# Two stacked transformer blocks on one core: grouped output products in a delta rule, first triangular blocks turned by TensorE, and waits placed elsewhere

## The reference, cut to what matters

```python
m = jnp.where(strict, jnp.einsum('bnhid,bnhjd->bnhij', kb, kc) * decay, 0.0)
...
sol = lax.linalg.triangular_solve(m, rhs, left_side=True, lower=True, unit_diagonal=True)
...
def step(state, xs):
    qd, kd, a, uu, ww, cd = xs
    v_new = uu - jnp.einsum('bhck,bhkv->bhcv', ww, state)
    o = jnp.einsum('bhck,bhkv->bhcv', qd, state) + jnp.einsum('bhij,bhjv->bhiv', a, v_new)
    state = state * cd[..., None, None] + jnp.einsum('bhck,bhcv->bhkv', kd, v_new)
    return state, o
```

## Time and profile before

| what | value |
|---|---|
| median of 3 runs | 2355.02 us (2354.6 to 2356.83) |
| profiled execution, its own time | 2357.62 us |
| its span, first to last instruction | 2355.8 us |
| TensorE busy | 2193.8 us (93%) |
| GpSimd busy | 1499.3 us (64%) |
| ScalarE busy | 1070.5 us (45%) |
| VectorE busy | 949.8 us (40%) |
| mean granted TensorE clock | 0.962 |

### The profile page before, as it was taken

One profiled execution on the slowest core, in us unless ns is written; L12 is line 12 of the kernel. 1 busy time (PEld: TensorE's weight loads), 2 busy tenths in 40 slices (PEclk: granted clock), 3 DMA queues, 4 the chain that ended last, 5 costly groups with the idle time before them and its releaser, 6 DMA issues.

```text
span 2355.8 us, 36004 instructions
## 1 busy us (share of the span) xinstructions
PE 2193.8 (93%) x15336; PEld 2010.8 (85%) x15336; DVE 949.8 (40%) x1528; ACT 1070.5 (45%) x1505; POOL 1499.3 (64%) x632
## 2 busy tenths in 40 slices
PE   7989989899878989989999899898999989998997
PEld 6779977799778879879899899888788789998997
DVE  4352356422375546375112211456374661123113
ACT  4555555455545252245444444462532444544443
POOL 6588876698844233356778688663243556686885
PEclk9999999999988989999999999999999999999999
DMA  8345534355522222243445455432122344454553
GB/s 326 126 161 183 193 116 161 108 197 181 185 92 102 68 70 77 72 143 129 149 164 186 143 186 190 143 126 83 61 90 72 116 139 158 144 179 147 193 179 117
DMA packets 47184, 333.06 MB, mean 141 GB/s; under 512 B 5168, under 2 KB 5552, under 8 KB 7856
## 3 DMA queue, kind: packets, MB, share of 16 engines
q1 hardware_dynamic: 47024, 330.76, 40.6%
HBM read 329.69 MB, written 1.05 MB: 140 GB/s over the span
## 4 chain that ended last, share of the span: by engine, by line
PE 61%; DVE 7%; ACT 3%; issue 1%; POOL 0%; ACTq 0%; DVEq 0%
PE bank L146 14%; PE bank L147 13%; PE bank L148 13%; PE y L146 2%; PE y L148 2%; PE y L147 2%; PE bank L1675 2%; PE bank L1611 1%; PE bank L1685 1%; PE bank L1729 1%; PE bank L1728 1%; DVE conv L1325 1%; PE bank L1684 1%; DVE sc L2285 1%; PE bank L1506 1%
## 5 line engine op out<-in xcount | busy, mean ns | idle before, releaser
L336 POOL TENSOR_TENSOR w_lo<-w_raw,w_hi 128x1024 fp32r<-128x1024 f32 x602 | 1465.7, 2440 | 831.7 <-ACT w_hi L327 831.7
L327 ACT ACTIVATE w_hi<-w_raw 128x1024 fp32r<-128x1024 f32 x602 | 636.4, 1059 | 1066.9 <-PE bank L148 896.3
L146 PE MATMUL bank<-x_hi,w_hi 128*128 128x256 f32 x2960 | 881.4, 298 | 34.0 <-POOL w_lo L336 19.3
L147 PE MATMUL bank<-x_lo,w_hi 128*128 128x256 f32 x2960 | 852.5, 288 | 0.0
L148 PE MATMUL bank<-x_hi,w_lo 128*128 128x256 f32 x2960 | 851.8, 288 | 0.0
L146 PEld LDWEIGHTS bank<-x_hi,w_hi 128*128 128x128 f32 x2960 | 583.3, 197 | 58.6 <-issue 24.3
L147 PEld LDWEIGHTS bank<-x_lo,w_hi 128*128 128x128 f32 x2960 | 583.4, 197 | 10.5 <-issue 8.6
L148 PEld LDWEIGHTS bank<-x_hi,w_lo 128*128 128x128 f32 x2960 | 582.7, 197 | 0.0
L862 DVE SCALAR_TENSOR_TENSOR conv<-bank,par_sb,conv 128x254 f32<-128x254 f32 (+1 forms) x176 | 76.8, 477 | 251.8 <-ACT conv L850 250.2
L1188 DVE TENSOR_TENSOR hid_lo<-hid,hid_hi 128x512 fp32r<-128x512 f32 x22 | 45.1, 2048 | 247.0 <-ACT hid_hi L1183 247.0
L146 PE MATMUL y<-w_hi,hid_hi 128*128 128x512 f32 x352 | 139.4, 396 | 1.2 <-DVE hid_lo L884 1.2
(11 more groups left out here) (393 smaller groups left out, 3279.8 us busy)
## 6 DMA issues: line engine op xcount, KB each, us to landing
w_raw<-w SPq DMA_DIRECT2D x300, 1024.0 KB, 4.8
ln_rows<-ln_rows SPq DMA_DIRECT2D x4, 1024.0 KB, 5.7
mem_tok<-mem SPq DMA_DIRECT2D x2, 1024.0 KB, 7.0
const_sb<-const SPq DMA_DIRECT2D x1, 1536.0 KB, 9.4
par_sb<-par SPq DMA_DIRECT2D x2, 553.5 KB, 10.7
xn<-xT SPq DMA_DIRECT2D x1, 1024.0 KB, 5.0
w_raw<-w SPq DMA_DIRECT2D x2, 512.0 KB, 5.3
x_tok<-x SPq DMA_DIRECT2D x1, 1024.0 KB, 8.5
```

Source lines behind the costliest of these rows:

```text
L146: pe.matmul(out, lhs[0], rhs[0], start=start, stop=False, skip_group_check=skip)
L147: pe.matmul(out, lhs[0], rhs[1], start=False, stop=False, skip_group_check=skip)
L327: act.activation(self.hi[:, h % HALVES, :], self.raw[:, n % RAWS, i * HW:(i + 1) * HW], ACT.Copy).then_inc(*sig.up("high", h))
L336: pool.tensor_tensor(self.lo[:, h % HALVES, :], self.raw[:, n % RAWS, i * HW:(i + 1) * HW], self.hi[:, h % HALVES, :].bitcast(F32), ALU.su ...
```

## The change

- In each output block of the scan the four heads' products with the state come first, then the four products with `vn`; only the first is marked as the start of an accumulation.
- The spread is two steps, `spread` (waits for the second key logarithm) and `spread_e` (waits for the fourth), with stream between them. Half 1's steps start one position later.
- `ti` (identity minus the first level of the triangle) is finished on DVE in the steps g0 and g1. TensorE turns `ti` instead of `mt`, and ScalarE copies the turned block to `t`, in place of three operations on DVE per group (one of them on `ti`, now made earlier).
- The gap before `tail0` is 4 instead of 2. ScalarE's table load and logarithms of the tail stand one position before `tail0`, instead of directly behind the last chunk.
- In the second mixer DVE's `normalise` of groups 0 and 1 stands ahead of `index_sum(1)`. The memory values' units and the gates and branches behind them use the banks in another order.
- In the first mixer the spread stands one half later, `scores(0)` and `turn(0)` one position later.

```diff
@@ -523,7 +523,7 @@
 
-        main.pe(pe, self.at(5))
+        main.pe(pe, self.at(6))
         if l == 0:
@@ -569,7 +569,7 @@
 
-        main.pe(pe, self.at(13))
+        main.pe(pe, self.at(13) + 1)
         pe.wait_ge(*sig.at("roped", l, 1))
@@ -582,7 +582,7 @@
         scores(3)
-        main.pe(pe, self.at(17))
+        main.pe(pe, self.at(17) + 1)
         turn(0)
@@ -1447,10 +1447,11 @@
         for c in range(2):
-            token_unit(f"mv{c}", m["mv"][:, :, c * HALF:(c + 1) * HALF], [4 + 2 * c, 5 + 2 * c], m["mn"])
+            token_unit(f"mv{c}", m["mv"][:, :, c * HALF:(c + 1) * HALF], [6 - 2 * c, 7 - 2 * c], m["mn"])
+        u["mv0"].need = u["mv0"].need + [("o_low", l, 1, 3)]
         for n in range(4):
-            gate_unit(1, n, 4)
-            branch_unit(1, n, 5)
+            gate_unit(1, n, 6)
+            branch_unit(1, n, 7)
         u["wb10"].need = u["wb10"].need + [("o_low", l, 1, 3)]
@@ -1465,7 +1466,7 @@
         self.units = [u[n] for n in self.order]
-        self.steps = [self.places(0, 30), self.places(1, 72)]
+        self.steps = [self.places(0, 30), self.places(1, 73)]
 
@@ -1479,10 +1480,10 @@
 
-        gaps = ([("spread", 0), ("k0", 4 if hf == 0 else 2), ("k1", 1), ("v0", 1), ("v1", 1), ("q0", 1), ("q1", 1), ("beta", 1),
+        gaps = ([("spread", 0), ("spread_e", 2 if hf == 0 else 1), ("k0", 2 if hf == 0 else 1), ("k1", 1), ("v0", 1), ("v1", 1), ("q0", 1), ("q1", 1), ("beta", 1),
                  ("g0", 1), ("g1", 1), ("lower", 2)] + [(f"{n}{lv}", 1) for lv in range(1, 6) for n in ("y", "c")]
                 + [("solved", 1)] + [(f"{n}{c}", g) for c in range(NCH) for n, g in (("w", 2), ("o", 1))]
-                + [("tail0", 2), ("tail1", 1)])
+                + [("tail0", 4), ("tail1", 1)])
         at, out = start, {}
@@ -1625,12 +1626,15 @@
         if hf == 0:
-            pe.wait_ge(*sig.at("key_logged", l, 0, 3))
+            pe.wait_ge(*sig.at("key_logged", l, 0, 1))
             pe.wait_ge(*sig.at("decays", l))
         else:
-            pe.wait_ge(*sig.at("key_logged", l, 1, 3))
+            pe.wait_ge(*sig.at("o_dn", l, 0, 0))
+        spread(m["rowq"][:, 1, :], 0).then_inc(*sig.up("spread_g", l, hf))
+        main.pe(pe, self.step_at(hf, "spread_e"))
+        pe.wait_ge(*sig.at("key_logged", l, hf, 3))
+        if hf:
             pe.wait_ge(*sig.at("o_dn", l, 0, 1))
-        spread(m["rowq"][:, 1, :], 0).then_inc(*sig.up("spread_g", l, hf))
         spread(m["ge_row"][:, :], 2).then_inc(*sig.up("spread_e", l, hf))
@@ -1663,14 +1667,14 @@
         for g in range(2):
-            pe.wait_ge(*sig.at("mt_made", l, hf, g))
+            pe.wait_ge(*sig.at("begun", l, hf, g))
             for n in range(4 * g, 4 * g + 4):
-                mm = pe.transpose(yd[g][:, (n % 4) * P:(n % 4 + 1) * P], h["mt"][:, n, :], K("ident"))
-            mm.then_inc(*sig.up("lower", l, hf, g, 0))
+                mm = pe.transpose(yd[g][:, (n % 4) * P:(n % 4 + 1) * P], h["ti"][:, n, :], K("ident"))
+            mm.then_inc(*sig.up("begun_turned", l, hf, g))
         for lv in range(1, 6):
             for g in range(2):
-                pe.wait_ge(*sig.at("kept", l, hf, g, lv - 1))
+                pe.wait_ge(*(sig.at("kept", l, hf, g, lv - 1) if lv > 1 else sig.at("t_begun", l, hf, g)))
                 for n in range(4 * g, 4 * g + 4):
@@ -1724,9 +1728,11 @@
             for hh in range(4):
-                cols = slice(hh * P, (hh + 1) * P)
-                pe.matmul(op[r, cols], h["qd"][:, hh, c * CH:(c + 1) * CH], h["st"][:, c % 2, hh, :], start=True, stop=False)
-                mm = pe.matmul(op[r, cols], h["at"][r, tt * 4 + hh, r], h["vn"][r, hh, :], start=False, stop=True)
+                pe.matmul(op[r, hh * P:(hh + 1) * P], h["qd"][:, hh, c * CH:(c + 1) * CH], h["st"][:, c % 2, hh, :],
+                          start=hh == 0, stop=False, skip_group_check=True)
+            for hh in range(4):
+                mm = pe.matmul(op[r, hh * P:(hh + 1) * P], h["at"][r, tt * 4 + hh, r], h["vn"][r, hh, :],
+                               start=False, stop=True, skip_group_check=True)
             mm.then_inc(*sig.up("o_done", l, hf, c))
@@ -1908,6 +1914,11 @@
         act.activation(h["e"][:, :, :], h["e"][:, :, :], ACT.Exp).then_inc(*sig.up("decay_made", l, hf))
+        main.act(act, self.step_at(hf, "lower"))
+        for g in range(2):
+            act.wait_ge(*sig.at("begun_turned", l, hf, g))
+            act.activation(h["t"][:, 4 * g:4 * g + 4, :], bank[g][:, :].rearrange("p (n i) -> p n i", n=4), ACT.Copy
+                           ).then_inc(*sig.up("t_begun", l, hf, g))
         main.act(act, self.step_at(hf, "solved"))
@@ -1927,6 +1938,7 @@
                                ).then_inc(*sig.up("o_squared", l, hf, tt))
+        main.act(act, self.step_at(hf, "tail0") - 1)
         act.preload_act_table_set("natural_log_exp_and_others")
@@ -2050,9 +2062,9 @@
         main.dve(dve, self.at(64))
-        self.index_sum(dve, 1)
         self.normalise(dve, 0)
         self.normalise(dve, 1)
+        self.index_sum(dve, 1)
         self.index_mask(dve, 1, {1: 66, 4: 69, 6: 70})
@@ -2179,6 +2191,11 @@
             dve.tensor_tensor(h["mt"][:, pr, :], heads(tt), h["es"][:, pr, :], ALU.mult).then_inc(*sig.up("mt_made", l, hf, tt))
+            dve.wait_ge(*sig.at("mt_made", l, hf, tt))
+            step(dve.tensor_tensor(h["ti"][:, pr, :], h["mt"][:, pr, :], K("level0T").unsqueeze(1).to_broadcast([P, 4, P]),
+                                   ALU.mult))
+            dve.tensor_tensor(h["ti"][:, pr, :], K("ident").unsqueeze(1).to_broadcast([P, 4, P]), h["ti"][:, pr, :],
+                              ALU.subtract).then_inc(*sig.up("begun", l, hf, tt))
 
@@ -2190,21 +2207,7 @@
 
-        for g in range(2):
-            pr = slice(4 * g, 4 * g + 4)
-            dve.wait_ge(*sig.at("mt_made", l, hf, g))
-            dve.tensor_tensor(h["ti"][:, pr, :], h["mt"][:, pr, :], K("level0T").unsqueeze(1).to_broadcast([P, 4, P]), ALU.mult
-                              ).then_inc(*sig.up("begun", l, hf, g))
         main.dve(dve, self.step_at(hf, "lower"))
-        for g in range(2):
-            pr = slice(4 * g, 4 * g + 4)
-            dve.wait_ge(*sig.at("begun", l, hf, g))
-            dve.tensor_tensor(h["ti"][:, pr, :], ident, h["ti"][:, pr, :], ALU.subtract)
-            dve.wait_ge(*sig.at("lower", l, hf, g, 0))
-            dve.tensor_tensor(h["t"][:, pr, :], four(g), lev[:, 0:1, :].to_broadcast([P, 4, P]), ALU.mult
-                              ).then_inc(*sig.up("masked2", l, hf, g, 0))
-            dve.wait_ge(*sig.at("masked2", l, hf, g, 0))
-            dve.tensor_tensor(h["t"][:, pr, :], ident, h["t"][:, pr, :], ALU.subtract).then_inc(*sig.up("kept", l, hf, g, 0))
         for lv in range(1, 6):
@@ -2216,7 +2219,7 @@
                 dve.wait_ge(*sig.at("cross", l, hf, g, lv))
-                dve.wait_ge(*sig.at("kept", l, hf, g, lv - 1))
+                dve.wait_ge(*(sig.at("kept", l, hf, g, lv - 1) if lv > 1 else sig.at("t_begun", l, hf, g)))
                 ins = dve.tensor_tensor(h["ti"][:, pr, :], h["ti"][:, pr, :], four(2 + g), ALU.subtract)
```

## The result

The changed kernel takes 2334.78 us (median of 4 runs, 2333.98 to 2336.76), the kernel before beside it on the same chip 2355.93 us: ratio 0.99, 95% interval 0.9884 to 0.9917. It is faster by about 21 us by the medians and by 23.6 us by the ratio (interval 19.6 to 27.3) where 56 were forecast, and 2334.8 lies outside the range of 2280 to 2326. The profiled execution of after took 2335.5 us (span 2333.4), 22.1 less than that of before.

The account below looks back on a forecast made before the run. TensorE, busy 93% of the span, bounds it by matmuls, waits and lower clock. Terms 13.5 + 11 + 14.1 + 2.9 - 4 - 1 + 10.1 + 3.5 + 6.0 = 56.1 us give 2299; range 2280 to 2326.

Parts of the forecast that it names:

- the first triangular blocks: Start of the triangular solve: turning a finished `ti` cuts waits from 13.0 to 2.9, plus 4 of clock: 14.1 us gained.
- the tail: Chain's end, `tail0` four positions behind: +2.9 us, less 4 at the index scores and 1 at half 1's rotations.
- the prediction's own signs of being wrong: Blocks keeping 0.36 us a product, 1.2 GHz behind shortened waits, or DVE waits beyond 3 us inside y and c steps.
- Grouping: Scan's 16 output blocks: one change of shape instead of seven, 2.88 to 2.04 us each, 13.5 us gained.
- Index order: Normalise ahead of the second index sum: 10.5 of wait and 4.8 of clock gone, new waits at `merged`; 10.1 us gained.
- First model: Spread a half later, scores and turn one position later: 6.0 us gained, with 3.0 lost at L512.
- Memory banks: Memory values in banks 6 and 7: the wait for mk3's copy goes, 3.5 us gained.
- Spread: Split spread, first group needing only the second key logarithm: wait 8.9 to 3.9, plus 6 of clock, 11 us gained.
- Clock: Time regained from TensorE's 1.2 GHz stretches behind waits that shrink or vanish, 19.8 us over all terms.
- waits move more than they vanish: Rival, chance 0.22: DVE is slow beside GpSimd at every named place, costing 17 us more, 2316 us.

Follow-up runs that it names:

- 8: The changed kernel with both the old tail (gap 2, logarithms straight behind the last chunk) and the old solve start (`mt` turned): 2313.65 us.
- 1: The kernel before with only the output products of the scan grouped: 2351.82 us.
- 9: The changed kernel with the new `ti` operations reading the Gram block in PSUM instead of SBUF, first triangular level left out: 2315.57 us.
- 10: The changed kernel with the old tail and three GpSimd weight subtractions a layer held back until DVE's steps are done: 2300.07 us.
- 11: As 10, but the second half's chain starts at position 72 as before, not 73: 2313.72 us.
- 6: The changed kernel with the old tail: gap 2 before `tail0`, table load and logarithms directly behind the last chunk: 2319.60 us.
- 3: The kernel before with only the spread split over two steps, the first waiting for the second key logarithm: 2349.25 us.
- 2: The kernel before with only both normalise steps moved ahead of the second index sum: 2347.83 us.
- 7: The changed kernel with the old solve start (`mt` turned, three DVE operations behind it, no ScalarE copy): 2325.17 us.
- 5: The kernel before with only the later tail: `tail0` four positions behind the last block, table load and logarithm one position ahead: 2386.93 us.

## Why the prediction was wrong

In the terms of the table the forecast had 13.5 for the work, 22.8 for waits and 19.8 for the clock. Measured, before against after: 2114.8 - 2103.6 = 11.2, 149.6 - 138.6 = 11.0, and half of 0.3 for the clock. Two steps make nearly all of the miss, the first triangular blocks and the tail: the forecast had 14.1 - 2.1 = 12 us gained for both, and undoing both (8) shows that they cost 18.8, 31 of the 32.5 us between forecast and measured gain. How the 31 divide depends on the order of undoing. Of the prediction's own signs of being wrong none came as written: the blocks take 2.04 us, the clock came back behind the shortened spread, and the wait beyond 3 us stands one step ahead of the y steps.

- **Grouping, 13.5: right.** 11.1 alone, 10.7 by the bookkeeping of single executions, 14.0 with the clock taken out of all of them. That the change of shape was the cost is argued, as said under 1. The Trainium skill, "TensorEngine Tiling (Array Packing)", "Key Properties", says that changing the tiling mode drains TensorE and gives no price; the blocks here agree with it, at 0.84 us for seven changes that became one.
- **Index order, 10.1: right** (8.7), with the new wait of 2.35 a layer where 2.1 stood. **First model, 6.0: right in sum** (6.8), wrong at L512, where DVE's shorter operation gave back what the forecast took, and wrong in the clock's 5.1, which did not come. **Memory banks:** the wait behind `mk` is gone as said; not run alone.
- **Spread, 11: measured 7.5.** The wait fell by 5.0 as forecast, and the clock gave about the 6 forecast (14 us less at 1.2 GHz between the medians); some 3 us came back, which no run explains.
- **First triangular blocks, 14.1: the step with the largest error in the changed kernel.** Undoing it gains 11.3, so it is off by 25; with the old tail it costs 0.5. The text priced the new operations as hidden, with "uncovered it costs up to 1 us a half, 4 in all". It had the right row, a pair of 3.26 us beside GpSimd, and placed it wrongly: it timed the last group's pair and its turn, and took the first group's to be clear. In the trace both groups meet a subtraction (2.78 and 2.72), the first one also delays the second group's `mt`, and TensorE waits 0.55 + 3.4 us in half 0 and 2.2 in half 1: 12.3 in all, 9.4 more than forecast. Runs 9 and 10 remove the wait in two different ways, by the operand's place and by GpSimd's timing, with DVE's list unchanged in number and order.
- **Tail, +2.9 - 4 - 1 = -2: the other step that failed.** Alone it costs 26.6 us, in the changed kernel 18.3, with the old solve start 7.5. Its own waits were sized right (z 6.2 as forecast, turns 8.1 against 7.0). Three things are off. The 5.5 us behind iq go by the later start of half 1 in any case (11 against 10), so their credit stood at the wrong edit; this makes no error in the sum, but the tail had nothing to set against its cost. At the index scores two operations of the rotation beside GpSimd took 2.69 and 2.71 us, so 10.7 instead of 4 us of wait; 6.7 of it stay with the old tail (6). And the clock: 17.1 us more at 1.2 GHz from the last chunk of half 0 to the spread of half 1, where the forecast had a gain of 1 us.
- **Clock, 19.8 in all: it does come back where a wait goes** (3 and 10 have 14 and 29 us less at 1.2 GHz than before between the medians on one chip; in 2 the 5 us are within the spread), **and it goes in other places.** The forecast gave the first sort of stretch a value and the second nearly none. The new solve start brings 33.5 us more at 1.2 GHz (changed kernel against 7), with waits that add up to nearly the same, 138.6 and 139.8.

Of the rivals, "waits move more than they vanish" named the cause, DVE slow beside GpSimd, and priced it at 17 us: 4 each at blocks, rotations and tail, 3.4 at the index scores, 2 in the first model. Waits alone cost 9.4 + 6.7 + 1.1 = 17.2 more, almost that sum. What put the time beyond 2316, and beyond the range, is the clock: the rival kept the 20 us of it. 2299 + 17.2 + 19.8 for the clock + 2.3 for grouping - 3.0 at L512 comes to 2335.3, measured 2334.8. That this is so close is luck: two smaller waits of the forecast that never came (1 at the y steps, 1.4 in the first model) would make it 2332.9.

The four parts run alone add up: 11.1 + 8.7 + 7.5 + 6.8 = 34.1, and with 3.5 (`mk`) and 5.5 (iq, by the later start) 43.1, against 42.4 for kernel 8, which is these and nothing else (each term is uncertain by 2 to 4 us, so the sum agrees better than it had to). The tail and the solve start don't add, to them or to each other.

The Trainium skill, "SBUF — State Buffer", "SBUF: two separate sides", has the rule that the prediction weighed and then set aside: a vector operation with two SBUF inputs and a GpSimd operation exclude each other. The trace agrees at every place looked at (2.78 and 2.72 us for DVE beside GpSimd, 2.79 for GpSimd behind DVE, 0.69 with one operand in PSUM or with GpSimd held). Its section "Who interferes with whom" has vector operations of one SBUF input contend as well when they run in a two-port mode; L717, 1.65 against 0.30 us, agrees, though no run here shows its mode.

**What stays open.** Which wait pulls the clock down is not settled. 11 against 10 has 2.1 us more of waits and, between the medians, 33 us more at 1.2 GHz; the new solve start brings most of its time at 1.2 GHz 70 us and more behind itself; and the executions of one kernel differ by 10 us (2291.1 and 2301.6 for 10, 2355.2 and 2366.5 for before on one chip). The bookkeeping tells how much a span lost to the clock, not why a given stretch began. A clean way to make `ti` without two SBUF operands, which would leave GpSimd alone, was not tried.

## What to carry to other kernels

Before an elementwise step is moved onto a chain that the bottleneck waits for, look at what GpSimd does at the new time, not at the old one: beside GpSimd, an operation with two SBUF operands can last until GpSimd's instruction is over and somewhat longer (2.7 to 2.8 us here, for 0.69). Cure it by a PSUM operand, or by making GpSimd wait, and then follow the backlog to the next place where such operations stand. Count a wait that disappears once, by the edit that removes it with the others undone, and price the clock behind a new wait as well as behind an old one, knowing that here it could not be placed from the waits alone.

## What the hardware showed that was not expected

- A vector operation of 128 x 4 with one input (TENSOR_SCALAR, L717) lasted until GpSimd's subtraction was over, 1.65 us when it began 0.76 us into it and 0.30 when 0.27 us of it were left: held like the large ones. The reduction just ahead of it (TENSOR_REDUCE, 128 x 512, one input) took the same 0.69 us beside that subtraction: not held.
- In the changed kernel every operation at L735, L1523, L1525 (`iq`), L2195 and L2197, all with both operands in SBUF, that starts within a subtraction of GpSimd ends 0.55 us after that subtraction.
- When GpSimd runs its subtractions back to back, each two-operand operation of DVE waits for one: 5 in 12.00 us.
- Products of 8 rows stand in many of the dropped stretches (spreads of 3.7 to 3.8 us instead of 1.99, in 5, in 11 and at 1700.93 in the changed kernel), each time with a wait or a run of small products ahead. No run separates the rows from what stands ahead of them.
